# Two decoder layers unrolled, expert rounds as one run-time loop, and one weight split moved

## Chip, cores and metric

The kernel runs on one core of a Trainium2 chip. The metric is the device time of one launch in microseconds (us), the median over runs.

## The reference, cut to what matters

Two layers (DEPTH = 2) of a decoder trunk over 512 tokens of width 1024, in float32:

```python
for l in range(DEPTH):
    proj = rms_norm(x, norm1_g[l]) @ w_in[l]            # 1024 -> 2560
    y_ret  = silu(r_g) * rms_norm(retention(rq, rk, rv))  # 4 heads
    y_moba = moba_attention(mq, mk, mv)                  # 4 heads
    y_mem  = memory_attention(cq, ck, cv)                # 4 heads, keys from
                                     # rms_norm(mem, mem_norm_g[l]) @ w_mem_kv[l]
    x = x + concat(y_ret, y_moba, y_mem) @ w_out[l]
    x = x + hier_moe(rms_norm(x, norm2_g[l]), ...)       # 16 experts, 2 per token
```

Each expert is `(silu(t @ w_gate) * (t @ w_up)) @ w_down` with 1024 -> 512 -> 1024.

## The kernel before, in words

**Precision.** Every float32 product of activations and weights is three fp32r matmuls: high half by high half, high by low, low by high (function `three`, L1386 to L1388). So each weight unit (128 x 1024) is loaded by a DMA of the SP queue into one of eight slots of `stage`, copied by ACT to a high half (`make_hi` L349, `expert_hi` L381) and subtracted by DVE to a low half (`make_lo` L390, `expert_lo` L386). SP's `load` (L407) waits until the low half of the unit eight places earlier is made. Counters (`s_hi`, `s_lo`, `s_used`) keep the units in one global order.

**Five programs.** SP, POOL, ACT, DVE and PE each run a program written out by hand, ordered by semaphores. Each program is a hardware loop over the two layers: `Fori(0, DEPTH)` at L470 (SP), L532 (POOL), L682 (ACT), L931 (DVE) and L1421 (PE). Layer-dependent addresses and counts come from registers, and what belongs to one layer alone (loading x, adding the results of the experts of the layer before) stands in a run-time `If` (L479, L542, L970).

**Attention part of a layer.** ACT squares the two tiles of `mem` (L688) and takes a root (L691); DVE takes the reciprocal (L951), scales `mem` with the gain `gvec` (L946) and makes the first low halves; PE turns `mem` (L1418) and multiplies. In the second layer DVE then adds the experts' rows to x (`combine`, L925), eight operations in four pairs. Projections follow. The attention loop has 24 steps, j = 0 to 23; PE fills its idle time in it with the last projection units (`fill`), of which unit 23 is the last. A unit's buffer becomes free during the loop at the steps of `FREED_AT`, the last at j = 23: there ACT makes the high half of unit 27, the fourth unit of the output weights, and behind it evacuates the last projection (`evacuate(4)`, with Silu, L727). DVE makes unit 27's low half (L1082, by L390) ahead of `tile_out(3)`, the last division by the row sums (L1054, L1055). PE waits for that division (L1532) before it turns the retention inputs. The retention loop (L1091, r = 0 to 7) follows, where DVE masks scores (L1096, L1097) in turn with PE.

**Experts part.** DVE routes the tokens and counts the largest number per expert; `rounds_i` is how many passes over 128 slots per expert are needed. With these inputs it is 1. `experts(first)` exists twice in each program: `experts(True)` for the first pass, and `experts(False)` in a loop behind `If(rounds > 1)` (L907 ACT, L1368 DVE, L1792 PE, L660 POOL, L497 SP). Inside, ACT, DVE and SP run the expert pairs by `turns`: a loop of three, one pair written out, a loop of three (L334, L337); PE and POOL have one loop of seven (L1773, L639). POOL gathers token rows to `xg` (L608) and scatters results to `pair_rows` (L619). A pass ends with `meet`: three engines report, POOL clears the semaphores and releases them.

**The turn from layer 1 to layer 2** on an engine is thus: `meet`, the branch over `experts(False)`, the layer loop's closing branch, the layer's first work. On POOL the first work is `gvec` (L540) and `g_norm1` (in `hd`, L541), then `load_results` (L530), which waits for the last scatter.

```python
rounds = experts(True)                 # L906
with sc.If(rounds > 1):
    with sc.Fori(1, rounds) as r:
        experts(False)
with sc.Else():
    sc.nop()
```

Of the kernel before, what the change touches and what calls it, by code (L numbers as in the profile page):

```python
# [63 lines left out]
def build(nc, a, out):  # L64
# [4 lines left out]
    with ctx:  # L69
# [24 lines left out]
        ss = sb("ss", [128, 16])  # L94
        rstd = sb("rstd", [128, 16])
# [307 lines left out]
        def _(sp):  # L403
# [16 lines left out]
            def load_pass(base0, first):  # L420
# [29 lines left out]
                e = sp.snap(flat[0] + (2 * TURN_E + 1))  # L450
# [13 lines left out]
                step(end, sp.snap(flat[0] + (E_N - 1)), U_FIRST)  # L464
                downs(end, sp.snap(flat[0] + (E_N - 1)), U_FIRST + U_E)
# [4 lines left out]
            with sp.Fori(0, DEPTH) as layer:  # L470
# [8 lines left out]
                with sp.If(layer < 1):  # L479
# [3 lines left out]
                with sp.Else():  # L483
                    sp.nop()
# [6 lines left out]
                flat[0] = sp.snap(layer * E_N)  # L491
# [19 lines left out]
        def _(pool):  # L511
# [8 lines left out]
            pool.reg_mov(passes, 0)  # L520
            pool.dma_start(spare[:, :], a["const_pack"][0:16, 0:2]).then_inc(s_yst[1], 16)
# [10 lines left out]
            with pool.Fori(0, DEPTH) as layer:  # L532
# [67 lines left out]
                def experts(first):  # L600
# [56 lines left out]
                    return rounds if first else None  # L657
# [11 lines left out]
        def _(sc):  # L669
# [6 lines left out]
            per_unit = 16 // NS  # L676

# [4 lines left out]
            with sc.Fori(0, DEPTH) as layer:  # L682
# [56 lines left out]
                for j in range(24):  # L739
# [72 lines left out]
                def experts(first):  # L812
# [1045 lines left out]
```

## Time and profile before

| what | value |
|---|---|
| median of 3 runs | 1258.1 us (1255.04, 1259.31, 1258.1) |
| profiled execution, its time | 1256.25 us |
| its span, first to last instruction | 1254.6 us |
| around the span | 1.65 us |
| granted TensorE clock, mean | 0.955 |
| PE busy | 1144.6 us (91%) |
| DVE / ACT / POOL busy | 897.5 / 698.4 / 186.5 us |
| DMA, mean | 221 GB/s |

All rows further down are from that one profiled execution. Starts are us from the start of its span. In the timelines the first number is the start, the second the length; the brackets say how long the engine was idle before and what ended that. A name such as ACTq is the sequencer of ACT: register operations, branches and semaphores, which are not counted as busy. In the chain of waits a piece called issue is time in which the engine waited for nothing that the profile shows.

### The profile page before, as it was taken

Reading aid. Unit: us, or ns where it says so; the run is one execution under the profiler, and the core shown is the slowest. Engines: PE = TensorE matmul, PEld = TensorE weight load, DVE = VectorE, ACT = ScalarE, POOL = GpSimd, SP = SyncE. Lnnn points to the kernel's source line nnn. Section 1 sums busy time; section 2 is a strip of 40 time slices with the busy share of each in tenths; the row PEclk is TensorE's granted clock in tenths of the full one; section 3 lists DMA queues with packets and bytes.
Section 4 is the critical chain, followed back from the end, with each engine's and each line's share of the span. In section 5 each row is a group of like instructions: output and inputs, shape, how many; then the busy total and the mean of one; then the engine's idle time right before and its main releaser. Section 6 shows DMA issues by size and latency. Waiting matters only on the chain.

```text
span 1254.6 us, 18217 instructions
## 1 busy us (share of the span) xinstructions
PE 1144.6 (91%) x5538; PEld 917.3 (73%) x5538; DVE 897.5 (72%) x1288; ACT 698.4 (56%) x968; POOL 186.5 (15%) x238
## 2 busy tenths in 40 slices
PE   4999998999999999999279999989999999999991
PEld 3887676788777887777168876667877788877770
DVE  5467555637988988988194675556489888988973
ACT  6322322324888888887252223324248888888860
POOL 3005001001012212211400050010011212222211
PEclk9999799999999999999679997999999999999996
DMA  9522211206999979997943222112089997999965
GB/s 341 185 82 67 68 34 34 68 34 249 365 368 351 358 266 377 369 361 295 340 147 102 69 66 68 34 35 84 34 296 375 373 371 270 344 365 381 364 241 213
DMA packets 121892, 277.46 MB, mean 221 GB/s; under 512 B 13265, under 2 KB 13473, under 8 KB 121680
## 3 DMA queue, kind: packets, MB, share of 16 engines
q1 hardware_dynamic: 106912, 240.30, 53.1%
q0 software_dynamic: 14896, 36.19, 8.0%
q8 instruction: 34, 0.56, 0.2%
q14 instruction: 50, 0.41, 0.1%
HBM read 269.56 MB, written 23.07 MB: 233 GB/s over the span
## 4 chain that ended last, share of the span: by engine, by line
PE 70%; DMA 11%; DVE 9%; issue 5%; ACT 3%; POOL 1%; POOLq 0%; ACTq 0%; DVEq 0%
PE bank L1386 19%; PE bank L1388 18%; PE bank L1387 18%; DMA xg<-h_scratch,tok_now 5%; DMA pair_rows<-ysb,pair_now 5%; PE bank L1418 3%; PE bank L1490 2%; PE bank L1717 2%; PE bank L1511 1%; PE bank L1517 1%; PE bank L1485 1%; DMA hd<-pair_rows 1%; PE bank L1575 1%; DVE w_lo L390 1%; DVE x L925 1%
## 5 line engine op out<-in xcount | busy, mean ns | idle before, releaser
L386 DVE TENSOR_TENSOR w_lo<-stage,w_hi 128x1024 fp32r<-128x1024 f32 x244 | 294.0, 1220 | 16.0 <-ACT w_hi L381 14.5
L381 ACT ACTIVATE w_hi<-stage 128x1024 fp32r<-128x1024 f32 x236 | 246.4, 1059 | 48.0 <-PE bank L1388 48.0
L1386 PE MATMUL bank<-w_hi,hT_hi 128*128 128x512 f32 x384 | 157.5, 410 | 4.5 <-DVE hT_lo L939 4.5
L1388 PE MATMUL bank<-w_hi,hT_lo 128*128 128x512 f32 x384 | 152.6, 397 | 0.0
L1387 PE MATMUL bank<-w_lo,hT_hi 128*128 128x512 f32 x384 | 152.5, 397 | 0.0
L386 DVE TENSOR_TENSOR more_lo<-stage,more_hi 128x1024 fp32r<-128x1024 f32 x124 | 146.0, 1218 | 1.8 <-ACT more_hi L381 1.4
L381 ACT ACTIVATE more_hi<-stage 128x1024 fp32r<-128x1024 f32 x124 | 127.9, 1060 | 15.0 <-PE bank L1388 14.5
L349 ACT ACTIVATE w_hi<-stage 128x1024 fp32r<-128x1024 f32 x56 | 58.8, 1057 | 113.9 <-PE bank L1388 113.9
L390 DVE TENSOR_TENSOR w_lo<-stage,w_hi 128x1024 fp32r<-128x1024 f32 x56 | 67.9, 1220 | 74.9 <-ACT w_hi L349 73.9
L1386 PE MATMUL bank<-w_hi,xgT_hi 128*128 128x512 f32 x264 | 104.7, 396 | 1.2 <-DVE xgT_lo L1282 1.2
L1387 PE MATMUL bank<-w_lo,xgT_hi 128*128 128x512 f32 x264 | 104.9, 397 | 0.0
L1388 PE MATMUL bank<-w_hi,xgT_lo 128*128 128x512 f32 x264 | 104.0, 394 | 0.0
L1386 PE MATMUL bank<-more_hi,xgT_hi 128*128 128x512 f32 x248 | 103.3, 417 | 0.0
L1386 PE MATMUL bank<-w_hi,hidT_hi 128*128 128x512 f32 x248 | 99.9, 403 | 3.0 <-DVE hidT_lo L1319 3.0
L1388 PE MATMUL bank<-w_hi,hidT_lo 128*128 128x512 f32 x248 | 98.6, 398 | 0.0
L1387 PE MATMUL bank<-w_lo,hidT_hi 128*128 128x512 f32 x248 | 97.9, 395 | 0.0
L1387 PE MATMUL bank<-more_lo,xgT_hi 128*128 128x512 f32 x248 | 97.8, 394 | 0.0
L1388 PE MATMUL bank<-more_hi,xgT_lo 128*128 128x512 f32 x248 | 97.7, 394 | 0.0
L1386 PEld LDWEIGHTS bank<-w_hi,hT_hi 128*128 128x128 f32 x384 | 73.8, 192 | 19.4 <-issue 5.8
L1388 PEld LDWEIGHTS bank<-w_hi,hT_lo 128*128 128x128 f32 x384 | 73.8, 192 | 16.0
L1387 PEld LDWEIGHTS bank<-w_lo,hT_hi 128*128 128x128 f32 x384 | 73.9, 192 | 13.7
L1308 DVE TENSOR_TENSOR xgT_lo<-bank,xgT_hi 128x512 fp32r<-128x512 f32 x60 | 38.6, 686 | 38.1 <-ACT xgT_hi L823 38.1
(239 smaller groups left out, 2009.5 us busy)
## 6 DMA issues: line engine op xcount, KB each, us to landing
stage<-in_w_exp_up SPq DMA_DIRECT2D x124, 512.0 KB, 5.8
stage<-in_w_exp_gate SPq DMA_DIRECT2D x122, 512.0 KB, 5.6
stage<-in_w_exp_down SPq DMA_DIRECT2D x122, 512.0 KB, 6.2
stage<-in_w_in SPq DMA_DIRECT2D x40, 512.0 KB, 4.2
stage<-in_w_out SPq DMA_DIRECT2D x16, 512.0 KB, 3.9
stage<-in_w_mem_kv SPq DMA_DIRECT2D x8, 512.0 KB, 7.5
h_scratch<-act POOLq DMA_DIRECT2D x8, 512.0 KB, 2.9
act<-pair_rows POOLq DMA_DIRECT2D x8, 512.0 KB, 6.2
```

The costliest lines, as they stand in the source:

```text
L349: eng.activation(w_hi[:, n % NW, :], stage[:, n % NS, :], ACT.Copy).then_inc(s_hi, 1)
L381: eng.activation(x_hi[n % NX], src, ACT.Copy).then_inc(s_hi, 1)
L386: eng.tensor_tensor(x_lo[n % NX], src, x_hi[n % NX].bitcast(f32), ALU.subtract).then_inc(s_lo, 1)
L390: eng.tensor_tensor(w_lo[:, n % NW, :], stage[:, n % NS, :], w_hi[:, n % NW, :].bitcast(f32), ALU.subtract).then_inc(s_lo, 1)
L925: dv.scalar_tensor_tensor(out=x[:, t, :], in0=y_rows[q], scalar=wtok[:, q % 2, t:t + 1], in1=x[:, t, :], op0=ALU.mult, op1=ALU.add).then_i ...
L1308: ins = dv.tensor_tensor(xgT_lo[:, i, 4 * q:4 * q + 4, :], bank[4 + q][:, :].rearrange("p (k c) -> p k c", k=4), xgT_hi[:, i, 4 * q:4 * q ...
L1386: pe.matmul(dst, l_hi, r_hi, start=start, stop=False)
L1387: pe.matmul(dst, l_hi, r_lo, start=False, stop=False)
L1388: return pe.matmul(dst, l_lo, r_hi, start=False, stop=stop)
L1418: ins = pe.transpose(bank[b][:, 128 * q:128 * q + 128], src(q), ident)
L1490: ins = pe.matmul(bank[j % 2][:, 0:128 * (t + 1)], hd[part_, 1, h // 2, tok], hd[part_, 2, h // 2, 0:128 * (t + 1)], start=True, stop=True)
L1717: ins = pe.transpose(bank[4 + k // 4][:, 128 * (k % 4):128 * (k % 4) + 128], xg[:, i, 128 * k:128 * k + 128], ident)
```

## The change

1. The layer loop of each of the five programs becomes a Python loop: both layers are written out, with the layer number a constant. The three layer-dependent `If`s disappear. SP's index registers for the expert addresses become constants outside the loops.
2. On POOL, ACT, DVE and PE the two copies of `experts` become one loop `Fori(0, rounds)`, whose body runs at least once. The register `rounds` is set to 1 ahead of it and to the true count near the end of the body. What a later pass needs besides stands at the start of the body in `If(r > 0)` with an `Else`. SP keeps its second copy behind `If(rounds > 1)`.
3. In the attention loop ACT leaves out unit 27's high half at j = 23, runs a Silu on one column (`tint`), evacuates the last projection, and makes the high half then. DVE makes the low half in the retention loop behind r = 5.

The diff, cut to its core (PE, DVE, ACT and POOL have the same loop edit):

```diff
@@ SP
-                e = sp.snap(flat[0] + (2 * TURN_E + 1))
+                e = flat[0] + (2 * TURN_E + 1)
...
-                        step(base, sp.snap(flat[0] + pair * 2 + (i + 1)), U_FIRST + U_E * i, aside)
+                        step(base, held(sp, pair * 2 + (flat[0] + i + 1)), U_FIRST + U_E * i, aside)
...
-            with sp.Fori(0, DEPTH) as layer:
+            for layer in range(DEPTH):
...
-                with sp.If(layer < 1):
+                if layer == 0:
...
-                flat[0] = sp.snap(layer * E_N)
+                flat[0] = layer * E_N
@@ POOL
-            with pool.Fori(0, DEPTH) as layer:
+            for layer in range(DEPTH):
...
-                with pool.If(layer > 0):
+                if layer > 0:
                     load_results()
-                with pool.Else():
-                    pool.nop()
...
-                def experts(first):
+                pool.reg_mov(rounds, 1)
+                with pool.Fori(0, rounds) as r:
...
-                    if first:
+                    with pool.If(r > 0):
+                        gather_dma(0, slot_tok[:, 0:1])
+                    with pool.Else():
                         pool.dma_start(spare[:, :], a["const_pack"][0:16, 0:2]).then_inc(s_xg[0], 16)
-                    else:
-                        gather_dma(0, slot_tok[:, 0:1])
                     gather_dma(1, slot_tok[:, 1:2])
-                    if first:
-                        pool.wait_ge(s_known, 1)
-                        rounds = rounds_of(pool)
+                    pool.wait_ge(s_rounds, layer + 1)
+                    apart(pool)
+                    pool.reg_mov(rounds, rounds_of(pool))
...
-                rounds = experts(True)
-                with pool.If(rounds > 1):
-                    with pool.Fori(1, rounds) as r:
-                        experts(False)
-                with pool.Else():
-                    pool.nop()
@@ ACT
-            with sc.Fori(0, DEPTH) as layer:
+            for layer in range(DEPTH):
...
-                    if j in FREED_AT:
+                    if j in FREED_AT and j < 23:
                         make_hi(sc, base, 20 + FREED_AT[j])
...
+                sc.activation(tint[:, :], eps, ACT.Silu)
                 evacuate(4)
+                make_hi(sc, base, 20 + FREED_AT[23])
...
-                def experts(first):
+                sc.reg_mov(rounds, 1)
+                with sc.Fori(0, rounds) as r:
...
-                    if not first:
+                    with sc.If(r > 0):
                         for n in range(NW):
                             expert_hi(sc, base_p, n)
+                    with sc.Else():
+                        sc.nop()
@@ DVE
-                steps = chain.n
-                with dv.If(layer > 0):
-                    before = dv.snap(layer * 16, min_val=16, max_val=16 * DEPTH)
-                    for t in range(NT):
-                        combine(before, t)
-                        if t:
-                            norm_x(t - 1)
-                with dv.Else():
-                    chain.n = steps
-                    for t in range(NT):
+                for t in range(NT):
+                    if layer > 0:
+                        combine(layer * 16, t)
+                    else:
                         dv.wait_ge(s_xin[t], 16)
                         dv.sem_inc(s_x, 4)
-                        if t:
-                            norm_x(t - 1)
+                    if t:
+                        norm_x(t - 1)
...
                 probs_out(23)
-                make_lo(dv, base, 20 + FREED_AT[23])
                 tile_out(3)
...
                         ins.then_inc(s_re, 1)
+                    if r == 5:
+                        make_lo(dv, base, 20 + FREED_AT[23])
...
+                dv.reg_mov(rounds, 1)
+                with dv.Fori(0, rounds) as r:
...
-                    if not first:
+                    with dv.If(r > 0):
                         for n in range(NW):
                             expert_lo(dv, base_p, n)
+                        first_rows_lo()
+                    with dv.Else():
+                        dv.nop()
@@ PE
-                    if first:
-                        pe.wait_ge(s_half_l, 1)
-                        gate_up(0, base_p, 0, 0, 4)
-                        pe.wait_ge(s_xgl, 1)
-                        gate_up(0, base_p, 4, 4, 2)
-                    else:
-                        turn_rows(0, p2 * 128 + 16)
-                        pe.wait_ge(s_xgl, 1)
-                        gate_up(0, base_p, 0, 0, 6)
+                    with pe.If(r > 0):
+                        pe.wait_ge(s_xg[0], p2 * 128 + 16)
+                        apart(pe)
+                        for k in range(KT):
+                            ins = pe.transpose(bank[2 + k // 4][:, 128 * (k % 4):128 * (k % 4) + 128],
+                                               xg[:, 0, 128 * k:128 * k + 128], ident)
+                            if k % 4 == 3:
+                                ins.then_inc((s_half_t, s_xgt)[k // 4], 1)
+                    with pe.Else():
+                        pe.nop()
+                    pe.wait_ge(s_half_l, 1)
+                    gate_up(0, base_p, 0, 0, 4)
+                    pe.wait_ge(s_xgl, 1)
+                    gate_up(0, base_p, 4, 4, 2)
```

## Rows read from the trace of the kernel before

**Rows 1.** Busy time by stretch: length, PE, PEld, DVE, ACT, POOL, granted clock, DMA share, GB/s

```profile
300.00:606.00 306.00, 299.30 (x1416) 240.68 (x1414) 266.75 (x284) 244.04 (x287) 53.99 (x61) 1.00 0.94 347
```

**Rows 2.** Timeline of PE at the turn from layer 1 to layer 2

```profile
627.28 3.67 PE L1418 MATMUL bank<-con,proj 128*128 128x128 f32 x16 [21.72 <-DVE proj L946]
```

**Rows 3.** Timeline of ACT at the same turn

```profile
620.36 1.28 ACT L688 ACT_TABLE_LOAD   x1 [13.93 <-issue]
...
625.29 0.29 ACT L691 ACTIVATE rstd<-ss,con 128x2 f32<-128x2 f32 x1
```

**Rows 4.** Chain of waits at the turn, in order of time: start, length, what

```profile
608.10 5.82 issue
613.91 0.04 ACTq L682
...
614.02 6.16 issue
...
647.64 1.30 DVE x L925
```

**Rows 5.** Branches by source line: ns min/median/max, first to last start, x count

```profile
L1792 PEldq COMPARE_BRANCH  x1: 5255/5255/5255, 608.1 to 608.1; - x1
...
L1773 PEldq COMPARE_BRANCH  x14: 83/215/239, 352.3 to 1193.8; - x14
...
L334 ACTq COMPARE_BRANCH  x1: 50/50/50, 355.3 to 355.3; - x1
L334 ACTq FUSED_REGOPS  x1: 106/106/106, 355.6 to 355.6; - x1
...
L970 DVEq COMPARE_BRANCH  x1: 67/67/67, 20.3 to 20.3; - x1
...
L980 DVEq EVENT_SEMAPHORE  x4: 21/21/21, 20.6 to 23.7; - x4
```

**Rows 6.** Timeline of POOL at the turn

```profile
607.53 1.02 POOL L619 DMA_INDIRECT pair_rows<-ysb,pair_now  x1 [0.86 <-DVEq L398]
609.62 0.58 POOL L540 DMA_DIRECT2D gvec<-in_mem_norm_g  x1 [1.07 <-issue]
...
615.65 2.09 POOL L530 DMA_DIRECT2D act<-pair_rows  x4 [4.88 <-DMA pair_rows<-ysb,pair_now]
```

**Rows 7.** DMA issues from 590 to 640 us: KB each, median us to landing

```profile
proj<-in_mem POOLq DMA_DIRECT2D x1, 1024.0 KB, 9.1
hd<-pair_rows POOLq DMA_DIRECT2D x2, 512.0 KB, 11.6
gvec<-in_mem_norm_g POOLq DMA_DIRECT2D x1, 512.0 KB, 6.7
```

**Rows 8.** Timeline of DVE at the turn

```profile
625.94 2.48 DVE L946 SCALAR_TENSOR_TENSOR proj<-proj,rstd,gvec 128x1024 f32<-128x1024 f32 x2 [0.15 <-DVE rstd L951]
...
635.27 2.59 DVE L925 SCALAR_TENSOR_TENSOR x<-act,wtok,x 128x1024 f32<-128x1024 f32 x2
```

**Rows 9.** Timelines of ACT, DVE and PE at the end of layer 1's attention loop

```profile
209.68 1.06 ACT L349 ACTIVATE w_hi<-stage 128x1024 fp32r<-128x1024 f32 x1 [5.84 <-PE bank L1388]
...
210.77 1.23 DVE L390 TENSOR_TENSOR w_lo<-stage,w_hi 128x1024 fp32r<-128x1024 f32 x1 [4.96 <-ACT w_hi L349]
...
207.21 1.00 PE L1517 MATMUL bank<-proj,probsT 128*128 128x64 f32 x8
...
212.89 3.36 PE L1418 MATMUL bank<-con,proj 128*128 128x128 f32 x16 [3.24 <-DVE act L1055]
```

**Rows 10.** The same place in layer 2, PE

```profile
834.08 3.38 PE L1418 MATMUL bank<-con,proj 128*128 128x128 f32 x16 [3.24 <-DVE act L1055]
```

**Rows 11.** Timeline of DVE in the retention loop, r = 6

```profile
228.12 0.42 DVE L1096 TENSOR_TENSOR probs<-bank,con 128x256 f32<-128x256 f32 x1 [1.54 <-PE bank L1555]
```

**Rows 12.** Timelines of PE and its weight loads at the start of layer 1's experts

```profile
307.39 0.49 PE L1386 MATMUL bank<-w_hi,xgT_hi 128*128 128x512 f32 x1 [0.61 <-DVE xgT_lo L1282]
...
315.90 0.86 PEld L1717 LDWEIGHTS bank<-con,xg 128*128 128x128 f32 x8 [0.29 <-DMA xg<-h_scratch,slot_tok]
```

More of the change, by code:

```diff
@@ L94, in build @@
         ss = sb("ss", [128, 16])
+        tint = sb("tint", [128, 1])
         rstd = sb("rstd", [128, 16])
@@ L895, in experts @@
                     hidden_hi(E_N)
-                    if first:
-                        sc.wait_ge(s_known, 1)
-                        rounds = rounds_of(sc)
+                    sc.wait_ge(s_rounds, layer + 1)
+                    apart(sc)
+                    sc.reg_mov(rounds, rounds_of(sc))
                     results(E_N, 0, end[0], U_FIRST + U_E + FT)
@@ L903, in experts @@
                     sc.reg_add(passes, passes, 1)
-                    return rounds if first else None
-                rounds = experts(True)
-                with sc.If(rounds > 1):
-                    with sc.Fori(1, rounds) as r:
-                        experts(False)
-                with sc.Else():
-                    sc.nop()
         @block.vector
@@ L919, in _ @@
             dv.reg_mov(passes, 0)
+            rounds = dv.alloc_register("dve_rounds")
             def combine(loaded, t):
@@ L929, in combine @@
                         dv.sem_inc(s_x, 4)
-            with dv.Fori(0, DEPTH) as layer:
+            for layer in range(DEPTH):
                 p = dv.snap(passes, min_val=0, max_val=NT * DEPTH)
@@ L1332, in step @@
                             expert_lo(dv, base_e, n0 + n, aside)
-                    if not first:
-                        rows_lo(0, 1)
                     for n in range(NW, U_FIRST + 3):
@@ L1351, in experts @@
                     hidden_lo(E_N)
-                    if first:
-                        rounds = rounds_of(dv)
+                    dv.reg_mov(rounds, rounds_of(dv))
                     dv.tensor_scalar(pos[:, :, :], pos[:, :, :], -128.0, None, ALU.add).then_inc(s_tail, 1)
@@ L1364, in experts @@
                     dv.reg_add(passes, passes, 1)
-                    return rounds if first else None
-                rounds = experts(True)
-                with dv.If(rounds > 1):
-                    with dv.Fori(1, rounds) as r:
-                        experts(False)
-                with dv.Else():
-                    dv.nop()
             for t in range(NT):
@@ L1382, in _ @@
             pe.reg_mov(passes, 0)
+            rounds = pe.alloc_register("pe_rounds")
             def three(dst, l_hi, l_lo, r_hi, r_lo, start, stop):
@@ L1419, in turn @@
                 ins.then_inc(s, 1)
-            with pe.Fori(0, DEPTH) as layer:
+            for layer in range(DEPTH):
                 p = pe.snap(passes, min_val=0, max_val=NT * DEPTH)
@@ L1707, in _ @@
                 slot_table(bank[6][:, 0:E_N * VALS], s_at, 2, s_tab)
-                def experts(first):
+                pe.reg_mov(rounds, 1)
+                with pe.Fori(0, rounds) as r:
                     p2 = pe.snap(passes, min_val=0, max_val=NT * DEPTH)
@@ L1781, in experts @@
                     down(E_N, end, U_FIRST + U_E)
-                    if first:
-                        pe.wait_ge(s_known, 1)
-                        rounds = rounds_of(pe)
+                    pe.wait_ge(s_rounds, layer + 1)
+                    apart(pe)
+                    pe.reg_mov(rounds, rounds_of(pe))
                     slot_table(bank[5][:, 0:E_N * VALS], s_tail_at, 1, s_tail_tab)
@@ L1788, in experts @@
                     pe.reg_add(passes, passes, 1)
-                    return rounds if first else None
-                rounds = experts(True)
-                with pe.If(rounds > 1):
-                    with pe.Fori(1, rounds) as r:
-                        experts(False)
-                with pe.Else():
-                    pe.nop()
 _INS = ["x", "mem", "norm1_g", "w_in", "ret_norm_g", "moba_qn_g", "moba_kn_g", "mem_norm_g", "w_mem_kv", "mem_qn_g",
```

47 lines of the change are left out of this document (22 added, 25 removed).

## The prediction

> **What bounds the kernel now.** I read the busy time by stretch first. Over the 306 us of layer 1's experts PE is busy 299.3 us at a granted clock of 1.00 [rows 1], and layer 2's experts look the same. Nothing in the change shortens matmul work, so a gain has to come from the few us in which PE stands. The timeline of PE shows where it stands longest: 21.72 us at the turn from layer 1 to layer 2 [rows 2]. It waits for DVE's scaling of `mem`, and DVE waits for ACT. The timeline of ACT says why ACT is late: its first work of layer 2 is a table load at 620.36, after 13.93 us in which it waited for nothing that the profile shows [rows 3]. The chain of waits splits that: 5.82 us behind the branch over the second copy of the experts, then the layer loop's closing operation at 613.91, then 6.16 us behind the layer loop's branch back [rows 4]. These are two far jumps. PE has one too, with the stall counted in the branch: 5255 ns at L1792 [rows 5]. Near jumps cost little. PE's seven-trip loop branches in 215 ns (14 records, median), ACT's pair loop gets from its branch at 355.3 to its next operation at 355.6, and DVE gets from the `If` at 20.3 over the combine code to 20.6 [rows 5]. Third, the end of the attention loop: PE stands 3.24 us in each layer until the last division [rows 9, 10].
>
> **Part 1, the turn.** The change removes both far jumps from ACT, DVE, PE and POOL: there is no second copy to leap, and layer 2's code stands right behind. The new loop's closing branch is not taken with one round, and the untaken branches of the trace (the 83 ns end of L1773's range) show no stall [rows 5]. So ACT can begin up to 5.82 + 6.16 = 12.0 us earlier, at 608.4 instead of 620.4. That is the upper bound. From ACT's table load to the end of its root it takes 625.58 - 620.36 = 5.2 us [rows 3], so the root is ready at 613.6 and DVE could scale `mem` at 614.0 instead of 625.94 [rows 8]. What is late next? First `mem` itself: the transfer of 9.1 us [rows 7], issued near 600.5, lands at 609.6, when the 1.28 us table load has just ended, so it costs nothing or a few tenths. Second the gain `gvec`: issued at 609.62 [rows 6], 6.7 us to landing [rows 7], so at 616.3 if nothing about it changes. That is the lower bound, a shift of 625.94 - 616.3 = 9.6 us. POOL's 1.07 us of idle time ahead of it [rows 6] holds its own two jumps and should shrink by some 0.7, and SP, which loses the jump back to its layer head, loads the first units of layer 2 some 3 us earlier, which unloads the queues. I take 615.0, a shift of 10.9 us.
>
> From the scaling to the first combine operation DVE needs 635.27 - 625.94 = 9.3 us, and the eight combine operations with the norms between end at 648.9 [rows 4, 8], 13.7 us after the first. With the shift they run from 624.3 to 638.0. Their inputs must keep up. `load_results` starts at 615.65, when the last scatter has landed [rows 6]; its last two transfers (`hd`) take 11.6 us [rows 7] from issues near 619, so the last lands near 631. The eighth operation needs it at 636.7. There are 5 to 6 us of room, which have to absorb the loads of `w_in` that follow DVE's earlier low halves: four units of 0.5 MB at the 347 GB/s of rows 1 are 6 us if they went ahead of everything. So at worst a few tenths are lost. PE's work on `mem` moves along with DVE. Part 1: 10.9 us gained, between 9.6 and 12.0.
>
> **Part 2, unit 27.** Now the order is: last fill on PE ends, ACT makes the high half (209.68), DVE the low half (210.77, 1.23 us), then the division, then PE at 212.89 [rows 9]. The division itself needs only the last values product, which begins at 207.21 and takes 1.00 us [rows 9]. Without the split DVE runs reciprocal and division from 208.3 to about 209.2, before the last fill ends at 209.65. PE goes on without a gap and all of the 3.24 us goes, in each layer: 6.5 us. PE next needs the evacuated last projection, 3.4 us of transposes later. Before, its four tiles ran behind the high half and a table load; now the table load is done under the last attention steps by `tint`, three tiles go before the last fill ends and the fourth right after it. POOL's multiplication by `g_ret` moves forward with them and nobody waits for it. The moved high half (1.06 us) finds ACT idle. The moved low half finds DVE behind r = 5 with 1.54 us of idle time before r = 6 [rows 11]; it takes 1.23, so it fits with 0.3 to spare. If it did not fit at all, DVE would be 1.2 us later per layer. Behind the low half only one SP load is queued, that of the unit eight places on; it is issued some 12 us later and needed 60 us later, by the high halves ahead of the experts. Nothing is queued behind it, since the next load waits for later low halves anyway. Part 2: 6.5 us, at least 4.0.
>
> **Part 3, the new branches.** At the start of each layer's experts POOL, ACT, DVE and PE now set a register, enter a loop and take the jump of `If(r > 0)` to its `Else`. A near jump is 0.2 to 0.3 us [rows 5]; with the extra register work I take 0.4 us per engine. ACT is idle there for several us. PE has 0.61 us before its first expert matmul, in which it waits for DVE's halves [rows 12], and the jump fits in it. DVE's jump stands behind those halves and its next product is needed some us later. POOL's comes straight ahead of the gather for expert 1, for which PE already waits 0.29 us [rows 12]. So 0.4 us is added there in each layer, 0.8 us in all, between 0 and 1.6. The Trainium skill prices such a branch lower (Advanced Engine Details and Errata, Control Flow Timing: about 108 ns for compare and branch); by that the loss would be 0.2 us instead of 0.8. The trace's 0.3 us from branch to target decides. The later read of `rounds` on each engine stands where it stood, with one semaphore increment more. SP's constants in place of registers shorten its issue path, but SP mostly waits for DVE: nothing.
>
> **Sum.** 10.9 + 6.5 - 0.8 = 16.6 us. Against the profiled execution's own 1256.25 us (span 1254.6 and 1.65 around it) that is 1239.7. The median of the three runs lies 1.9 us higher; I meet it half way and say 1240.5. The bounds of the parts together give gains from 9.6 + 4.0 - 1.6 = 12.0 to 18.5 us, so 1237.8 to 1244.3; the runs scatter by some 2 us about their middle. About 0.3% (4 us) is what a measurement of this kernel can tell from no change.
>
> **Rivals.** (a) One stall stays. Straight-line code is fetched ahead during attention, where no engine shows such a stall, but the entry into layer 2 follows a loop's end and may still pay one fetch of about 6 us on ACT. Against it speaks that the pair loops' exits show none. Part 1 would then give 5 us, the time 1246.4. Chance 0.11.
> (b) The new `If` on PE is a far jump after all. For it: the body is repacked and 16 instructions are leapt. It costs 5.3 us [rows 5], less the 0.6 of cover, in each layer: 9.4 us back, 1250. Chance 0.06.
> (c) Slower. The inner pair loops of ACT or DVE lose their cheap branch back. Writing out two layers gives each of these loops a new place in the code. If a loop straddles a boundary of what the engine holds, its four branches back per layer cost 5.8 us like the far jump [rows 4] instead of 0.3. ACT runs ahead of PE by a few units at most, so perhaps 3.5 of that reaches PE: 8 x 3.5 = 28 us lost in both layers, the time 1268. It decides for slower than before from 16.6 / 8 = 2.1 us per branch. The profile speaks against it: two pair loops each on ACT, DVE and SP and one each on PE and POOL, in both layers, all branch back cheaply, and they can't all lie well by luck. The Trainium skill speaks for it (Runtime: NRT & Kernel Launch, Instruction fetch mechanics): an engine holds only two pages of instructions, fetched strictly forward, and a taken branch outside of them waits for a fetch; by that a loop whose tail pulls in a third page would miss at each trip. The far jumps agree with that rule, and no row shows a loop that breaks. Chance 0.05.
> (d) The change does not do what it says at the turn, since the transfers (`gvec`, scatter, results) land no earlier than before and `w_in` crowds them: that is the lower bound of part 1, inside the forecast.
>
> **How the numbers follow.** The forecast has 0.76, rivals (a) to (c) 0.22, and 0.02 is left for a gain that something unseen cancels. The range is 1235.0 to 1248.0: it holds the forecast with its bounds and the runs' scatter, and rival (a); (b) and (c) are left out. Faster: the forecast, (a) and (b), 0.93. Same: 0.02. Slower: 0.05.
>
> **What the changed profile would show.** ACT's idle time ahead of its first table load of layer 2 should fall from 13.9 us to about 2, PE's from 21.7 to about 11, and DVE's scaling should start when `gvec` lands. The gap of 3.24 us before the transposes should vanish in both layers, and r = 6 should start no later behind r = 5. PE's wait for the first gather should grow from 0.3 to 0.7 us. Wrong would be: a stall of 5 us or more on a branch of the new loop or `If`, pair loops with pauses at each trip, or DVE waiting for the result rows in the combine.

## The result: 1.3% slower, and the profile after

The changed kernel takes 1274.93 us (median of 4 runs, 1265.01 to 1279.06) against 1257.03 us for the kernel before, a ratio of 1.013 with a 95% interval of 1.0067 to 1.0194. The forecast was 1240.5 us. The profiled execution took 1279.06 us with a span of 1277.3, so the rows below are of the slowest of the four.

The places that the change was about did what was forecast. First the turn to layer 2: ACT, then POOL, DVE and PE, from their timelines. Layer 1's experts end at 621.8 here and at 605.3 before.

```profile
621.82 1.09 ACT L839 ACTIVATE ysb<-bank 128x512 f32<-128x512 f32 x2 [8.23 <-PE bank L1367]
625.94 1.06 ACT L680 ACTIVATE probs<-proj 128x1024 bf16<-128x1024 f32 x1 [3.03 <-DMA proj<-in_mem]
...
625.15 0.58 POOL L540 DMA_DIRECT2D gvec<-in_mem_norm_g  x1
...
631.33 2.48 DVE L933 SCALAR_TENSOR_TENSOR proj<-proj,rstd,gvec 128x1024 f32<-128x1024 f32 x2 [1.26 <-DMA gvec<-in_mem_norm_g]
...
632.67 3.67 PE L1397 MATMUL bank<-con,proj 128*128 128x128 f32 x16 [10.64 <-DVE proj L933]
```

ACT has no stall without a cause left; it waits for `mem` (3.03 us) where it stood 13.93 us before [rows 3]. DVE's last wait is now `gvec`. PE stands 10.64 us, not 21.72 [rows 2]. From the end of layer 1's experts to PE's first projection it takes 662.2 - 621.7 = 40.5 us, before 656.8 - 605.3 = 51.5: 11.0 us gained.

Second the end of the attention loop (PE, layers 1 and 2), and DVE with the moved low half. The 3.24 us ahead of the transposes are gone in both layers [rows 9, 10], and the 16 transposes themselves take 1.91 us instead of 3.36 and 3.38. The low half fits ahead of r = 6, for which DVE still waits 0.40 us [rows 11].

```profile
208.76 0.39 PE L1367 MATMUL bank<-w_hi,hT_lo 128*128 128x512 f32 x1
209.00 1.91 PE L1397 MATMUL bank<-con,proj 128*128 128x128 f32 x16
...
836.95 1.91 PE L1397 MATMUL bank<-con,proj 128*128 128x128 f32 x16
```

```profile
221.58 1.22 DVE L391 TENSOR_TENSOR w_lo<-stage,w_hi 128x1024 fp32r<-128x1024 f32 x1
223.20 0.42 DVE L1076 TENSOR_TENSOR probs<-bank,con 128x256 f32<-128x256 f32 x1 [0.40 <-PE bank L1534]
```

Third the branches. PE's new `If` (first row) and its pair loop's branch back (second row) show no stall like the 5255 ns of before [rows 5]. ACT's pair loop (third row) has none either.

```profile
L1742 PEldq COMPARE_BRANCH  x2: 232/238/243, 302.5 to 930.5; - x2
...
L1758 PEldq COMPARE_BRANCH  x14: 76/208/217, 354.9 to 1217.6; - x14
...
L335 ACTq COMPARE_BRANCH  x6: 40/45/45, 359.6 to 1059.5; - x6
```

The loss is where the prediction had looked only once. Busy time by stretch for both layers' experts, the kernel before first, then the changed one with two short stretches behind a stall (columns as in [rows 1]):

```profile
307.40:605.30 297.90, 292.25 (x1341) 233.90 (x1342) 261.28 (x264) 241.97 (x283) 53.99 (x61) 1.00 0.94 346
928.60:1226.30 297.70, 293.76 (x1343) 234.97 (x1344) 261.24 (x264) 241.96 (x283) 55.99 (x61) 0.99 0.92 340
```

```profile
304.00:621.80 317.80, 297.35 (x1342) 242.08 (x1343) 261.52 (x264) 242.73 (x283) 65.39 (x61) 0.96 0.89 326
932.00:1250.10 318.10, 296.31 (x1341) 240.94 (x1341) 261.42 (x264) 242.54 (x283) 66.38 (x61) 0.97 0.86 316
353.00:358.00 5.00, 4.99 (x16) 4.31 (x17) 1.86 (x3) 2.45 (x4) 0.02 (x1) 0.50 0.48 180
358.00:363.00 5.00, 5.00 (x22) 4.04 (x22) 3.52 (x4) 4.12 (x5) 1.95 (x2) 0.94 0.49 147
```

The same instructions need 317.80 and 318.10 us instead of 297.90 and 297.70: 40.3 us lost. POOL is busy 11.4 and 10.4 us longer per layer, with the same 61 instructions. What PE waits for, in total (us, times, longest):

```profile
PE bank L1697 <- DMA xg<-h_scratch,tok_now: 34.9, 11, 4.4
PE bank L1397 <- DVE proj L933: 24.5, 2, 13.9
```

```profile
PE bank L1418 <- DVE proj L946: 35.7, 2, 21.7
PE bank L1418 <- DVE act L1055: 6.5, 2, 3.2
...
PE bank L1717 <- DMA xg<-h_scratch,tok_now: 3.5, 9, 1.0
```

The second fence is the kernel before. The wait for the gathered rows `xg` grew from 3.5 to 34.9 us. After each long stall the granted clock is 0.50, the lower of TensorE's two levels, for 3 to 7 us. The stretch 353 to 358 lies in one of the longer ones, and matmuls start 0.43 us apart in it. The rounded clocks of the two expert stretches give 0.04 x 317.8 + 0.03 x 318.1 - 0.01 x 297.7 = 19 us more for that. The gather's own rows say where it starts (POOL by tile `xg`: ns min/median/max; before, then after):

```profile
L608 POOL DMA_INDIRECT xg<-h_scratch,tok_now x28: 1135/1751/1865, 312.9 to 1185.0; - x28
```

```profile
L607 POOL DMA_INDIRECT xg<-h_scratch,tok_now x28: 1113/1746/5161, 309.9 to 1203.9; - x28
```

Same median, another maximum: 8 of the 28 issues take 4.01 to 5.16 us, and the 8 long waits of PE follow them. One of them, beside DVE's instructions one by one:

```profile
341.43 5.15 POOL L607 DMA_INDIRECT xg<-h_scratch,tok_now  x1 [0.86 <-POOL tok_now L604]
...
341.04 1.22 DVE L387 TENSOR_TENSOR w_lo<-stage,w_hi 128x1024 fp32r<-128x1024 f32 x1
...
342.17 1.22 DVE L387 TENSOR_TENSOR more_lo<-stage,more_hi 128x1024 fp32r<-128x1024 f32 x1
...
343.31 1.23 DVE L387 TENSOR_TENSOR more_lo<-stage,more_hi 128x1024 fp32r<-128x1024 f32 x1
344.44 1.22 DVE L387 TENSOR_TENSOR w_lo<-stage,w_hi 128x1024 fp32r<-128x1024 f32 x1
345.76 1.23 DVE L387 TENSOR_TENSOR w_lo<-stage,w_hi 128x1024 fp32r<-128x1024 f32 x1
...
353.01 1.97 PE L1697 MATMUL bank<-con,xg 128*128 128x128 f32 x8 [4.25 <-DMA xg<-h_scratch,tok_now]
```

### The profile page after: what moved, and what is told of

Same layout as the page of the kernel before. It is cut to its first block, busy times and chain, and to the rows that moved or that the text cites. A ratio compares the mean times of both kernels' runs of the same rounds, so it can differ in the third digit from the quotient of the medians.

```text
span 1277.3 us, 17886 instructions
## 1 busy us (share of the span) xinstructions
PE 1152.0 (90%) x5538; PEld 931.7 (73%) x5538; DVE 897.7 (70%) x1288; ACT 701.3 (55%) x971; POOL 208.5 (16%) x238
## 4 chain that ended last, share of the span: by engine, by line
PE 65%; DMA 17%; DVE 9%; issue 4%; ACT 2%; POOL 1%; POOLq 0%; SPq 0%; DVEq 0%; ACTq 0%
PE bank L1365 17%; PE bank L1366 16%; PE bank L1367 16%; DMA xg<-h_scratch,tok_now 8%; DMA pair_rows<-ysb,pair_now 5%; PE bank L1397 2%; PE bank L1697 2%; PE bank L1469 2%; PE bank L1490 1%; PE bank L1496 1%; PE bank L1464 1%; PE bank L1600 1%; ACT ysb L839 1%; DMA hd<-pair_rows 1%; DMA xg<-h_scratch,slot_tok 1%
## 5 line engine op out<-in xcount | busy, mean ns | idle before, releaser
L1365 PE MATMUL bank<-more_hi,xgT_hi 128*128 128x512 f32 x248 | 105.9, 427 | 0.0
L1367 PE MATMUL bank<-more_hi,xgT_lo 128*128 128x512 f32 x248 | 100.3, 404 | 0.0
```

The lines of the kernel that those rows point to most:

```text
L1365: pe.matmul(dst, l_hi, r_hi, start=start, stop=False)
L1367: return pe.matmul(dst, l_lo, r_hi, start=False, stop=stop)
```

## The experiments

The theory at the outset: `tint` alone makes the loss, by moving the tiles. The rival: the new loop form or the order of layer code makes it. Each kernel was timed against the kernel before on the same chip. "Long" is a gather issue over 2 us, counted in the profiled execution; the "pace" is the mean distance of two expert matmuls there, over some 1000 starts of layer 1 (before 0.2334 us, changed 0.2293).

**e1, e2: the tile taken out, and the tile alone.** e1 is the changed kernel with the table load's activation writing into the old tile `warm`:

```diff
-        tint = sb("tint", [128, 1])
...
-                sc.activation(tint[:, :], eps, ACT.Silu)
+                sc.activation(warm[:, :], eps, ACT.Silu)
```

e2 is the kernel before with the line of `tint` and nothing else; nobody writes or reads the tile.

> The changed kernel without the new one-column tile: the early Silu writes the existing tile warm instead, so every tile behind it keeps the address that it has in the kernel before. Theory A (the 4 bytes per partition of the new tile shift all later tiles, PE's expert matmuls follow each other at 0.229 us in place of 0.233, DVE's subtractions then run without gaps, and POOL's gather issue, which took 1.15 to 1.76 us before and up to 5.16 us after, is kept waiting): the matmul spacing goes back to 0.233 us, no gather issue is over 2 us, PE stands under 1.1 us at each gather, and the time is 1257.0 - 11.0 (turn) - 6.8 (attention) = 1239 us, between 1236 and 1243. Theory B (the new places of the expert loops in the code, or the run-time loop around them, make the gather late): nothing changes against the changed kernel, 1265 to 1280 us, with gather issues of 5.15 us.

> The kernel before with the one-column tile allocated at the same place and used by nothing. Theory A: the spacing of the expert matmuls falls to 0.229 us, a good part of the gather issues takes 4 to 5.16 us, PE stands some 4 us at each of those, and the time rises by up to 40 us, at least by 8: 1265 to 1297. Theory B: no difference, 1255 to 1259 us.

e1: 1237.61 us (1234.19 to 1240.04), ratio 0.9831 (0.9798 to 0.9864), no long gather, pace 0.2333. e2: 1279.92 us (1268.23 to 1284.01), ratio 1.0187 (1.0149 to 1.0226), 5 long gathers, pace 0.2291. An unused tile costs 1.9%; without it the change gains 1.7%. The rival falls.

**e3, e4: the parts of the change, each without the tile.** e3 leaves unit 27 where it stood before (high and low half ahead of the division) and keeps the written-out layers and the rounds loop. e4 is the kernel before with the split and the early table load into `warm`:

```diff
-                make_lo(dv, base, 20 + FREED_AT[23])
...
+                    if r == 5:
+                        make_lo(dv, base, 20 + FREED_AT[23])
```

> The changed kernel with the attention part as before: no tile, no early Silu, unit 27's halves at their old places. Layers unrolled and one run-time loop for the experts stay. Theory A: only the turn's 11.0 us are gained and some tenths are lost at the new branches, 1246 us, between 1243 and 1249. Theory B: the loss of about 40 us in the experts is all there and the attention gain is missing, 1272 to 1285 us.

> The kernel before with the attention part of the change alone, the early Silu written to the existing tile warm, so no address moves; layer loops and both copies of the experts stay. Theory A and theory B alike: 3.4 us less in each layer, 1250 us, between 1248 and 1252, with the expert matmuls at 0.233 us. A third theory C (an earlier start of the experts shifts DVE against POOL, whatever the addresses and the code): gather issues over 2 us appear here too and the time is above 1253.

e3: 1244.28 us (1240.87 to 1247.58), ratio 0.9902 (0.9865 to 0.9939), which on 1258.17 us is 12.3 us gained. e4: 1250.65 us (1245.25 to 1254.24), ratio 0.993 (0.9908 to 0.9952): 8.8 us. Together 21.1, and e1 with both gained 21.3 (17.1 to 25.4 by its interval): the parts add up.

**e5, e6: other addresses.** e5 adds a tile `pad` of 15 columns ahead of the large tiles of the changed kernel; e6 gives e1 one of a single column there.

```diff
         pair_now = sb("pair_now", [128, 2, 1], i32)
...
+        pad = sb("pad", [128, 15])
         with ExitStack() as part:
             pq = {c: sb(f"proj{c}", [128, NT, CH], scope=part) for c in (0, 1, 4, 3)}
```

```diff
         pair_now = sb("pair_now", [128, 2, 1], i32)
+        pad = sb("pad", [128, 1])
```

> The changed kernel with its one-column tile, and a second unused tile of 15 columns ahead of the large tiles of the experts part. The small tiles between the two (slot_tok and tok_now, which the gather reads, among them) stay shifted by 4 bytes; the large ones (xg, xgT_hi, xgT_lo, hidT_hi, hidT_lo) are shifted by 64 bytes. Theory A1 (the 4-byte shift of the large tiles quickens PE's expert matmuls, and the denser DVE work that follows keeps POOL's gather waiting): spacing 0.233 us, no gather issue over 2 us, 1238 us. Theory A2 (the shifted small tiles slow the gather itself): gather issues up to 5.15 us, 1265 to 1280 us.

> The changed kernel without its tile (the early Silu writes warm) and with an unused tile of one column ahead of the large tiles: only these are shifted by 4 bytes, the small ones are where they were. Theory A1: spacing 0.229 us, gather issues up to 5.15 us, 1265 to 1280 us. Theory A2: no gather issue over 2 us, and 1228 to 1238 us.

These two expectations count bytes of the tiles; the real shift goes in steps of 32. Against the kernel before, e5 has the small tiles moved by 32 bytes and the large ones (`xg`, `xgT`, `hidT`) by 96, e6 only the large ones by 32. e5: 1237.73 us (1232.1 to 1241.53), ratio 0.9829 (0.9773 to 0.9885), 2 long gathers, pace 0.2276. e6: 1241.54 us (ten executions, 1232.81 to 1254.84) against 1256.37 for the kernel before, none long in the profiled execution (1233.56 us), pace 0.2292. Neither theory foresaw this pair: e5 has a faster pace and two long gathers where none was expected, and e6 lies far below the 1265 to 1280 us that its pace should have brought. e6's times spread over 22 us, e1's over 6, so the long gathers seem to come and go from one execution to the next, though only one of e6's was profiled. The pace goes with the address of the large tiles.

**e7: gaps for POOL.** The changed kernel with its tile, and DVE waits for its own former low half to end ahead of two of them.

```diff
                         for n in range(7, U_E + 2):
+                            if n in (8, 9):
+                                dv.wait_ge(s_lo, base_e + (n0 + n + NS))
                             expert_lo(dv, base_e, n0 + n, aside)
```

> The changed kernel, tile and all, with two more waits in each of DVE's expert steps: the second and third subtraction behind the hidden layer's low half wait until the one before them is complete, so that DVE stands some 0.15 us ahead of each. Theory A1, second half (the gather issue gets on only when DVE leaves a gap between operations that read two SBUF tensors): the long gather issues become 1.7 to 3 us, PE stands less than 1.5 us at each gather, and with the quicker matmuls the time is 1228 to 1240 us. If DVE's density is not what holds the gather up: issues of 5.15 us stay, and the time is 1270 to 1285 us.

1232.22 us (1230.52 to 1235.66), ratio 0.9808 (0.9759 to 0.9857): the loss is gone in all four executions, with all tiles still moved. The pace stays 0.2292 and no gather is long:

```profile
L607 POOL DMA_INDIRECT xg<-h_scratch,tok_now x28: 1116/1746/1866, 308.9 to 1161.9; - x28
```

**e8: DVE made gapless at the old addresses.** e1 with three small subtractions per expert between low halves.

```diff
+                            if n < 10:
+                                two = con[:, 0:192]
...
+                                ins = dv.tensor_tensor(scr[:, n - 7, :], two, two, ALU.subtract)
```

> This kernel is the changed one with the activation of `Silu` writing into `warm` and no tile `tint`, so that every tile lies as in the kernel before, and with one small subtraction more on DVE (128x192, two inputs in SBUF, result into a scratch tile) ahead of each of the third to fifth low halves of an expert. It leaves no output out. Theory (a gather's issue on POOL is held while DVE runs two-input operations without a gap): the extra operations fill the 0.17 us gaps behind ACT, the matmuls keep the spacing of 0.2333 us, and still some gathers of `xg` take 4 us or more on POOL; the time is 1240 to 1275 us. Rival (the place of the tiles makes the long gathers by itself, DVE's gaps have no part): all gathers stay below 2 us and the time stays near the 1237.6 us of the same kernel without the extra operations.

1238.19 us (1235.93 to 1238.34), ratio 0.9844 (0.9819 to 0.9868), no long gather. DVE had no gap around most gathers (4.77 us in one piece at 341.86), and yet. But the small operations (0.35 us) also add boundaries between instructions, so this did not decide.

**e9 to e11: three more placements.** e9 is e1 with a `pad` of 16 columns ahead of the large tiles and e7's waits; e10 is e1 with e7's waits; e11 is e1 with `warm` allocated behind `pair_now`, which moves the small tiles between by 32 bytes down.

```diff
+        pad = sb("pad", [128, 16])
...
+                            if n in (8, 9):
+                                dv.wait_ge(s_lo, base_e + (n0 + n + NS))
```

```diff
-        warm = sb("warm", [128, 1])
...
         pair_now = sb("pair_now", [128, 2, 1], i32)
+        warm = sb("warm", [128, 1])
```

> The changed kernel without `tint`, with 64 bytes left free per partition ahead of the large tiles, and with DVE's waits that keep a gap between two low halves. Theory (the address of the large tiles sets the matmuls' pace, DVE's gaps keep the gathers short, and the two are independent): matmul spacing 0.2277 us in the experts, no gather over 2 us, 1226 to 1232 us, the shortest time of all. Rival (the faster pace makes the gathers long whatever DVE does): gathers over 4 us again, 1238 us or more.

> The changed kernel without `tint`, tiles as in the kernel before, with DVE's waits that keep a gap. Theory: the gathers were already short there, so the waits change nothing: spacing 0.2333 us, 1235 to 1240 us, as the same kernel without the waits (1237.6 us). Rival (the waits themselves are what gains, by another order on DVE): 1232 us or less at the same spacing.

> The changed kernel without `tint`, with `warm` allocated behind `pair_now`: the small tiles between lie 4 bytes lower, all large ones as in the kernel before. Theory (the place of the large tiles alone counts): spacing 0.2333 us, no gather over 2 us, 1235 to 1240 us. Rival (the place of `tok_now`, which the gather reads, counts): gathers of 4 us and more, 1245 us or more.

e9: 1234.21 us (1231.97 to 1237.91), ratio 0.9806 (0.9778 to 0.9833), pace 0.2333: the time lies 2 us above the expected range, and the pace is not the 0.2277 that was to bring it. e10: 1237.37 us (1232.98 to 1239.82), ratio 0.9828, pace 0.2334. e11: 1239.23 us (1237.12 to 1240.06), ratio 0.9847, pace 0.2334. None has a long gather. The addresses in the built programs explain e9's pace. `xgT_hi` starts at these bytes of its partition (e12 to e15, described below, are in the table too):

| kernel | start of `xgT_hi` | beyond a multiple of 128 | pace, us | long gathers |
|---|---|---|---|---|
| before, e1, e3, e4, e8, e10, e11, e12 | 180000 | 32 | 0.2333 to 0.2335 | none |
| e9, e15 | 180064 | 96 | 0.2332, 0.2333 | none |
| changed | 180032 | 64 | 0.2293 | 8 |
| e2, e14 | 180032 | 64 | 0.2291, 0.2292 | 5, 5 |
| e6 | 180032 | 64 | 0.2292 | none in this execution |
| e7 (with gaps) | 180032 | 64 | 0.2292 | none |
| e5 | 180096 | 0 | 0.2276 | 2 |
| e13 (with gaps) | 180096 | 0 | 0.2276 | none |

A pad of 64 bytes changes nothing; at a multiple of 64 PE is faster, at one of 128 a little more. The long gathers stand only in rows of a faster pace. `xg`, `sil`, `hid`, `hidT` and `ysb` move together with `xgT`, so the next batch had to part them.

**e12: a whole operation more on DVE, old addresses.** e1 with one 128x1024 subtraction behind the third low half, which adds length and no short pieces.

```diff
+            scr = sb("scr", [128, D], scope=part)
...
+                            if n == 7:
+                                two = con[:, 0:D]
+                                dv.wait_ge(s_dve, m + (chain.n - 1))
+                                dv.tensor_tensor(scr[:, :], two, two, ALU.subtract).then_inc(s_dve, 1)
```

> The changed kernel without `tint` (all tiles as in the kernel before) with one whole subtraction more on DVE (128x1024, two inputs in SBUF, into a scratch tile behind all others) behind the third low half of an expert, the place at which the long gathers stood. No output is left out. If a gapless DVE is enough for a long gather: several gathers of 4 us and more, 1245 us or more. If the place of the large tiles is needed too: all gathers below 2 us and 1236 to 1241 us, as the same kernel without the subtraction (1237.6 us).

1236.58 us (1235.68 to 1237.74), ratio 0.9831 (0.9791 to 0.987), no long gather. Its timelines of POOL and DVE at one gather:

```profile
414.03 1.74 POOL L607 DMA_INDIRECT xg<-h_scratch,tok_now  x1 [0.86 <-POOL tok_now L604]
...
413.65 1.22 DVE L387 TENSOR_TENSOR w_lo<-stage,w_hi 128x1024 fp32r<-128x1024 f32 x1
...
414.78 1.22 DVE L1321 TENSOR_TENSOR scr<-con 128x1024 f32<-128x1024 f32 x1
...
415.92 1.22 DVE L387 TENSOR_TENSOR more_lo<-stage,more_hi 128x1024 fp32r<-128x1024 f32 x1
...
418.19 1.22 DVE L387 TENSOR_TENSOR w_lo<-stage,w_hi 128x1024 fp32r<-128x1024 f32 x1
```

DVE's starts lie 0.38 us before the gather and 0.75, 1.89 and 4.16 after it, as in the long case at 341.43 (0.39 before, 0.74, 1.88 and 4.33 after), and the gather takes 1.74 us. 16 gathers of this execution have such starts and no gap, and none is long. One execution alone would prove little, as e6 shows, but e12's four lie within 2.1 us and e8's four within 2.4, so none of them had the loss. At the old addresses a gapless DVE is not enough.

**e13: the fastest place with the gaps.** e1 with a `pad` of 24 columns and e7's waits.

```diff
+        pad = sb("pad", [128, 24])
...
+                            if n in (8, 9):
+                                dv.wait_ge(s_lo, base_e + (n0 + n + NS))
```

> The changed kernel without `tint`, with 96 bytes ahead of the large tiles (so that `xg`, `xgT` and `hidT` start at a multiple of 128 bytes) and DVE's waits for a gap. If the pace of the matmuls goes by where these tiles start: spacing 0.2277 us, no gather over 2 us, 1225 to 1231 us. If the pace of the earlier run at this place (0.2277 us) was chance: 0.2333 us and 1235 to 1239 us.

1235.88 us (1234.41 to 1236.58), ratio 0.9823 (0.9784 to 0.9862). The pace is 0.2276 and no gather is long, so the address sets the pace again; the time expected from it did not come. The costliest groups show the pace as the mean duration of one matmul (ns, after the busy time): the kernel before, the changed one, e13.

```profile
L1387 PE MATMUL bank<-w_lo,xgT_hi 128*128 128x512 f32 x264 | 104.9, 397 | 0.0
```

```profile
L1366 PE MATMUL bank<-w_lo,xgT_hi 128*128 128x512 f32 x264 | 104.1, 394 | 0.0
```

```profile
L1368 PE MATMUL bank<-w_lo,xgT_hi 128*128 128x512 f32 x264 | 102.7, 389 | 0.0
```

And e13's busy time by stretch for layer 1's experts tells where the gain went:

```profile
302.90:599.10 296.20, 288.81 (x1340) 235.94 (x1341) 260.32 (x264) 241.94 (x283) 51.35 (x61) 0.99 0.95 351
```

Some 1150 expert matmuls per layer at 0.0057 us less are 6.6 us. PE's busy time falls by 3.4 us and the stretch by only 1.7, at a granted clock of 0.99 instead of 1.00 and with DMA at 351 GB/s: most of what a faster PE gains it then spends standing still.

**e14, e15: the operands alone, and the large tiles put back.** e14 puts 32 bytes between `xg` and `xgT_hi` in e1. e15 is the changed kernel, `tint` included, with 32 bytes ahead of the large tiles.

```diff
             xg = sb("xg", [128, 2, D], scope=part)
+            sb("pad", [128, 8], scope=part)
             xgT_hi = sb("xgT_hi", [128, 2, KT, 128], f32r, scope=part)
```

```diff
         tint = sb("tint", [128, 1])
...
+        pad = sb("pad", [128, 8])
         with ExitStack() as part:
             pq = {c: sb(f"proj{c}", [128, NT, CH], scope=part) for c in (0, 1, 4, 3)}
```

> The changed kernel without `tint`, with 32 bytes between `xg` and `xgT_hi`: `xgT` and `hidT` (what PE loads as weights in the experts) start at a multiple of 64 bytes, `xg` and all small tiles stay where they are. If the matmuls' pace goes by where PE's own operands start: 0.2292 us. If it goes by `xg` or the small tiles: 0.2333 us. For the gathers: some over 4 us if the faster pace is what makes them long, 1233 to 1255 us; else none.

> The changed kernel as it is, `tint` included, with 32 bytes more ahead of the large tiles alone: the small ones, `tok_now` among them, stay moved, the large ones start 32 bytes beyond a multiple of 64 again, as in the kernel before. If the large tiles' place is the cause of the loss: spacing 0.2333 us, no gather over 2 us, 1235 to 1240 us. If the place of `tok_now` or another small tile is: gathers of 4 us and more, 1260 us or more.

e14: 1256.71 us (1239.07 to 1267.45), against 1258.41 for the kernel before; the runs lie so far apart that no ratio is given. Pace 0.2292, 5 long gathers:

```profile
L607 POOL DMA_INDIRECT xg<-h_scratch,tok_now x28: 1117/1745/5160, 306.0 to 1185.3; - x28
...
  DMA xg<-h_scratch,tok_now: 46.3, 24
```

e15: 1236.72 us (1231.49 to 1241.12), ratio 0.9844 (0.9796 to 0.9893), pace 0.2332, none long:

```profile
L608 POOL DMA_INDIRECT xg<-h_scratch,tok_now x28: 1114/1747/1867, 306.9 to 1162.0; - x28
...
  DMA xg<-h_scratch,tok_now: 13.8, 25
```

The last line of each is the idle time of PE and its weight loads until a gather had landed (us, times). `xg` and `tok_now` are cleared: e14 has both at their old place and shows the loss, e15 has `tok_now` moved and shows none. What counts is the group `xgT`, `sil`, `hid`, `hidT`, `ysb`; PE loads `xgT` and `hidT` as weights.

**When an issue ends.** The traces also show what a long issue is. In all 17 profiles each of the 476 issues of this gather ends either 1.00 us (within 0.04) after the start of a DVE instruction or 0.9 us after DVE has begun a gap; of instants picked at random near them, some 9% do. e12's issue above ends 0.99 us after the start at 414.78. A long issue has let two or three such starts pass. The one of 4.01 us in the changed kernel ends 0.99 us after the third, the ones of 5.15 us end behind DVE's first gap:

```profile
558.78 4.01 POOL L607 DMA_INDIRECT xg<-h_scratch,tok_now  x1 [0.85 <-POOL tok_now L604]
...
561.80 2.56 DVE L387 TENSOR_TENSOR w_lo<-stage,w_hi 128x1024 fp32r<-128x1024 f32 x2
```

**Where it stands.** Shown: the loss is made by 32 bytes, through long gather issues. They need two things at once, that group at a multiple of 64 bytes and DVE without a gap: e12 has the second alone, e7 the first with gaps made, and neither has any. Not settled: why an issue passes over DVE's starts at the one place of the tiles and not at the other. With the same DVE starts and no gap up to 4.2 us after the gather's start, 8 of 9 gathers were long in the changed kernel, 5 of 11 in e14, none of 14 in e6 and none of 16 in e12, so chance, or something that differs between executions, has a part. The fixed versions (e1, e7, e9, e10, e13, e15; ratios 0.981 to 0.984) can't be told apart, and all beat both kernels. The simplest is e1.

## Why the prediction was wrong

**The step that failed** stands in its first paragraph: "Nothing in the change shortens matmul work, so a gain has to come from the few us in which PE stands", with the experts of 306 us taken as fixed [rows 1]. The line `tint = sb(...)` was part of the diff and got no price, not even a bound. Both halves of the sentence failed: PE's matmuls came 0.0041 us closer together, and the experts, taken as fixed, took 40.3 us longer through PE's waits for late gathers. Measured, that line costs 1.9% in the kernel before (e2: 1279.92 against 1258.17, 21.8 us) and 37 us between the medians of the changed kernel (1274.93) and e1 (1237.61).

**Part 1, the turn**: forecast 10.9 us between 9.6 and 12.0, measured 11.0 in the two traces and 12.3 in e3 (7.7 to 17.0 by its interval). The order of the waits was right too, with `gvec` last. **Part 2**: forecast 6.5 us, measured 8.8 (6.0 to 11.6 by e4's interval). The gap was the 3.24 us of [rows 9, 10], but a term was missing beside it: the clock behind the gap. In the kernel before, the transposes behind it ran at half clock, in the changed kernel at the full one (stretches of layers 1 and 2 before, then layer 1 after; columns as in [rows 1]):

```profile
213.00:216.00 3.00, 3.00 (x16) 3.00 (x16) 1.63 (x3) 1.12 (x3) 3.00 (x3) 0.53 0.52 175
834.00:837.00 3.00, 2.92 (x14) 2.93 (x15) 1.47 (x4) 1.30 (x3) 3.00 (x3) 0.50 0.53 175
```

```profile
209.00:212.00 3.00, 2.98 (x33) 2.57 (x31) 2.37 (x4) 1.55 (x2) 1.53 (x2) 1.00 0.00 0
```

The prediction read their 3.4 us as a fixed length. They take 1.91 us without the gap, 1.5 us less in each layer, and 6.5 + 2.9 = 9.4 is close to e4's 8.8. **Part 3**: forecast 0.8 us lost. The idle time of PE and its weight loads, added, until the first gathers had landed went from 0.6 us in the kernel before to 1.5 in e1, 0.9 more; of the weight loads alone it went from 0.6 to 1.1. The two overlap, so 0.9 is an upper bound. The sum forecast 16.6; e1, the change without its tile, gained 21.3, and its 1237.61 us lie inside the range of 1235.0 to 1248.0. So the reading of the turn and of the branches was sound, and the missing clock term went the favourable way.

**The rivals.** (a) No stall stayed at the turn. (b) The `If` is near: 238 ns. (c) Slower than before was right as a sign and wrong as a mechanism: PE's pair loop branches back in 208 ns (215 before), and each of ACT's 16 branches in the changed trace is followed by ACT's next operation within 1 us, where the two far jumps had cost 5.8 and 6.2. The Trainium skill's rule on two pages of instructions (Runtime: NRT & Kernel Launch, Instruction fetch mechanics) fits those far jumps; no run here shows a loop that breaks by it. (d) The transfers came in time.

**The balance of the two profiled spans** is 1277.3 - 1254.6 = 22.7 us. Layer 1's experts begin 3.4 us earlier; from their end to layer 2's experts it takes 310.2 us instead of 323.3; the tail takes 27.2 instead of 28.3. That is 17.6 gained, close to the forecast, and 40.3 lost in the experts. In these, 31.4 us are waits for gathers, 19 the clock, and the faster pace gives back 2304 x 0.0041 = 9.4; that makes 41, an estimate, since a part of each slow stretch lies inside the wait.

The clue was in the profile before. PE waited 9 times for a gather, at most 1.0 us: no slack was left. A gather issued late by 3.4 us had nothing to hide in. The prediction passed over this row, whose total of 3.5 us is small. The row shows that a late gather would cost its full delay; it does not show that one would come.

## What to carry to other kernels

A new tile is a change of every tile behind it. Before blaming logic, build the kernel before with the tile alone, and look at the addresses of the operands that the busiest engine reads. Allocate new small tiles last, or pad, and where POOL issues a gather while DVE runs two-input operations back to back, make DVE leave it a gap, as e7 did. (Issuing the gather earlier may help too; that was not tried.) A transfer that PE already waits for by 1 us is a transfer without slack.

## What was not expected of the hardware

- The distance between fp32r matmuls of 128x512 goes by the place of their operands: 0.2333 us at 32 or 96 bytes beyond a multiple of 128, 0.2292 at 64, 0.2276 at 0 (one profiled execution each; all 17 kernels fit). Matmuls on `xgT` and matmuls on `hidT` changed alike, from 0.2335 and 0.2334 to 0.2293 and 0.2291 in the changed kernel; the two were not moved apart.
- A gather issue on POOL takes 1.1 to 2.0 us, or, held up, 3.9 to 5.2 us. All 476 end 1.00 us after the start of a DVE instruction or 0.9 us after DVE's gap begins; those of 4.9 us and more are of the second kind.
- Each of the eight gather stalls of 3.2 to 4.4 us was followed by 3 to 7 us at half the clock. By the estimate of 19 us above, each cost 2.4 us more than its length. The 3.24 us ahead of the transposes had the same effect: 3.36 us for 16 transposes that take 1.91 at full clock.
